# Expert rounds of a diffusion trunk on one core: where column pieces, gathers and turns stand on TensorE, an unrolled loop, and two smaller edits

## The chip, the core and the metric

The program runs on one core of a Trainium2 chip. The core has five engines that run their own instruction queues and meet only at semaphores: TensorE (PE in the profile; PEld is its weight load), VectorE (DVE), ScalarE (ACT), GpSimd (POOL) and SyncE (SP, which here issues nearly all loads). The metric is device time in microseconds of one execution, lower is better. All data is float32.

## The reference, cut to what matters

One inference step over two groups of 128 tokens (context and latent), width 1024, four layers. Each layer has a token mixer (layers 0 and 3: gated DeltaNet; 1: short convolution; 2: neighbourhood attention) and a channel mixer: a dense SwiGLU in layers 0 and 2, and eight SwiGLU experts with two chosen for each token in layers 1 and 3.

```python
def moe_ffn(h, router, w_gu, w_down):
    logits = (h @ router).astype(jnp.float32)
    top_v, top_i = lax.top_k(logits, TOP_K)                       # 2 of 8
    w = jax.nn.softmax(top_v, axis=-1)
    combine = jnp.sum(jax.nn.one_hot(top_i, N_EXPERTS, dtype=jnp.float32) * w[..., None], axis=-2)
    gu = jnp.einsum('btd,edf->btef', h, w_gu)                     # 1024 x 2*1408 for each expert
    g, u = jnp.split(gu, 2, axis=-1)
    act = jax.nn.silu(g) * u * combine[..., None].astype(h.dtype)
    return jnp.einsum('btef,efd->btd', act, w_down)               # 1408 x 1024 for each expert

def dense_ffn(h, w_gu, w_down):
    g, u = jnp.split(h @ w_gu, 2, axis=-1)
    return (jax.nn.silu(g) * u) @ w_down
```

In the DeltaNet mixer, `g` is summed along each chunk (`g = jnp.cumsum(...)`), and differences of these sums go through an exponential into the decay matrix. After each channel mixer comes a gated residual and, ahead of the next mixer, an RMS norm.

## The kernel before

**The expert layers.** Each of the two runs eight rounds, one for an expert. In a round the tokens of that expert are gathered (`gather`: multiplications of the token rows with a selection matrix into banks 7 and 2 of the accumulator, which ACT and DVE then copy into `xg`), multiplied with the expert's gate and up weights, gated, turned, and multiplied with the down weights. Rounds 0, 2, 4 and 6 hold up to 96 tokens (`body`), rounds 1, 3 and 5 up to 64 (`small`), and what is left over goes through `wide` with 128. A round's weights are 1408 gate and 1408 up columns and 1408 down rows.

They lie in eleven slots of a ring. Slots 0, 4, 6 hold 384 gate columns each (`GATE`), 1, 5, 7 the up columns (`UP`), 8, 9, 10 three blocks of 128 down rows each, and slots 2 and 3 (`GATE_D`, `UP_D`) the last 256 gate or up columns together with one block of down rows. In a `body` round the matmuls on 384 columns use three of the four 32-column strips of the array, and the fourth strip works on the last 256 columns at the same time: so `columns(q, 0, ...)`, the first piece of a round, already needs slot 2, and the second needs slot 3 (`landed(q, j_d)`).

SP issues the loads of the next round in the fixed order 0, 1, 4, 5, 2, 3, 6, 7, 8, 9, 10, each as soon as TensorE has counted the slot free (`p_gu` counts column pieces, `p_dn` down pieces). There is one set of slots, so a load is issued while the round before is still computed, and SP stands at the first slot that is not free.

**The order on TensorE** is the order of the program. In `body` it is: columns of piece 0, columns of piece 1, `turn(0)`, `down(0)`, columns of piece 2, `turn(1)`, `down(1)`, both gathers for the next round, `turn(2)`, `down(2)`, `down(3)`. `turn(s)` transposes the gated block `s` (three transposes into bank 6); ACT copies it to `ma_T` and raises `a_at`; `down(s)` waits for that copy. So there is a wait for ACT wherever `down(s)` stands right behind `turn(s)`. In `small` the four column pieces are followed by `turn_small(0)`, `down_small(0)`, both gathers, `turn_small(1)`, `down_small(1)`. Round 0 is straight code, rounds 1 to 4 are two turns of a hardware loop (`pe.Fori(1, NARROW - 2, 2)`, one `small` and one `body` in a turn), rounds 5 and 6 are straight code again. ACT and DVE have loops of the same shape.

**The dense layers.** The last `down` adds into banks 2 to 5 in order (`k` 0 to 7, two to a bank) and raises `unit_done` at its end. DVE waits for this and then makes the residual bank by bank (`residual`, four instructions each, `xT`), ACT squares each finished bank for the norm, and TensorE sums the squares.

**DeltaNet.** `s_gc` makes, for one head, four 128x128 blocks whose rows all hold the running sum of the gates: a multiplication of a broadcast column of `G_` with a triangular matrix. The same running sums are in `GC` by then. DVE reads the blocks in `s_dec` (line 1985).

## Time and profile before

| what | value |
|---|---|
| median of 3 runs | 2390.7 us (2389.5 to 2394.16) |
| the profiled execution, its own time | 2388.28 us |
| its span | 2386.4 us |
| TensorE busy in it | 2247.8 us (94%) |
| DVE / ACT / POOL busy | 483.6 / 394.4 / 66.9 us |
| mean granted TensorE clock | 0.976 of full speed |
| moved by DMA | 551.00 MB, 231 GB/s over the span |

The profiled execution is 2.4 us below the median of the runs; 1.9 us of its own time lie outside its span. The expert rounds of layer 1 lie between 790 and 1202 us, those of layer 3 between 1979 and 2376 us. The dense layers end at 644 and 1645 us, and the DeltaNet cores lie between 192 and 365 us and between 1781 and 1912 us.

How to read the rows below. A timeline row has the start of a group of instructions, the time from its first start to its last end, engine, line, operation, shapes and count; the bracket is the idle time of the engine just before and what ended it. Nearly all matmuls pass through one helper and so have line 636; a float32 multiplication shows as two records there, a transpose as one. Turns have the lines 1134, 1135, 1173, 1175, 1236 and 1275. A row of windows has, for a stretch, its length and the busy time of each engine, then the granted TensorE clock, the share of the DMA engines and GB/s. "issue" is a wait that no semaphore in the profile explains.

### The profile page before, as it was taken

The page shows a single profiled execution, that of the slowest core. Times are in us where ns is not written, and L with a number is a line of the kernel's source. Part 1 is how long each engine was busy: PE and PEld are TensorE (multiplying, and loading weights), DVE is VectorE, ACT ScalarE, POOL GpSimd, SP SyncE. Part 2 cuts the span into 40 slices and gives each one's busy share as a digit, 9 for nine tenths or more (in the row PEclk, how much of TensorE's full clock was granted, in tenths as well). Part 3 has the DMA queues.
Part 4 walks back from the last instruction along what each step waited for, and adds up shares of the span by engine and source line. Part 5 has one row for each costly group of instructions (what it writes and reads, how often), then busy time and mean ns, then how long its engine had stood idle before and what let it go on. Part 6 is the DMA issues. An engine that isn't in the chain of part 4 may idle for free.

```text
span 2386.4 us, 44001 instructions
## 1 busy us (share of the span) xinstructions
PE 2247.8 (94%) x19595; PEld 1615.6 (68%) x19595; DVE 483.6 (20%) x1376; ACT 394.4 (17%) x819; POOL 66.9 (3%) x109
## 2 busy tenths in 40 slices
PE   7999998999999998999999999999998989989998
PEld 4776666888888544445576578888878875444455
DVE  2234332000112400000111420002344423000002
ACT  1133223000100100000112320001143331000001
POOL 4000001000000000000000000000000000000000
PEclk8999999999999999999999899999999989999999
DMA  8967888743355499999575696413440056999991
GB/s 323 279 226 280 304 312 270 211 153 115 106 168 203 158 384 353 368 380 382 206 237 193 223 258 185 139 36 108 142 138 7 12 177 246 386 369 373 380 389 56
DMA packets 355915, 551.00 MB, mean 231 GB/s; under 512 B 11280, under 2 KB 311184, under 8 KB 343232
## 3 DMA queue, kind: packets, MB, share of 16 engines
q1 hardware_dynamic: 344352, 525.31, 63.3%
q0 software_dynamic: 5840, 18.11, 2.9%
q10 hardware_dynamic: 5536, 4.73, 0.6%
q8 instruction: 160, 2.62, 0.5%
q14 instruction: 27, 0.22, 0.0%
HBM read 537.64 MB, written 14.93 MB: 232 GB/s over the span
## 4 chain that ended last, share of the span: by engine, by line
PE 88%; DVE 5%; ACT 3%; issue 2%; DMA 2%; ACTq 0%; SPq 0%; DVEq 0%
PE ps L636 86%; ACT ring L1437 1%; ACT work L1437 1%; DMA ring<-in_moe_w_down 1%; DVE ring L2003 0%; DVE work L1844 0%; DVE ring L1985 0%; DVE ring L2008 0%; DVE ring L1993 0%; DMA ring<-in_ada_w 0%; PE ps L1134 0%; PE ps L1027 0%; DVE ring L2011 0%; DVE xT L1862 0%; PE ps L662 0%
## 5 line engine op out<-in xcount | busy, mean ns | idle before, releaser
L636 PE MATMUL ps<-ring,work 128*32 128x384 f32 (+6 forms) x7752 | 698.3, 450 | 50.5 <-ACT work L1437 24.3
L636 PE MATMUL ps<-hT,ring 128*128 128x256 f32 x3200 | 713.2, 382 | 3.4 <-DVE hT L1854 3.2
L636 PEld LDWEIGHTS ps<-hT,ring 128*128 128x128 f32 x3200 | 608.4, 191 | 112.9 <-issue 12.2
L636 PEld LDWEIGHTS ps<-ring,work 128*32 128x32 f32 (+2 forms) x7752 | 336.1, 115 | 388.8 <-issue 264.1
L1437 ACT ACTIVATE work<-ps 128x256 f32<-128x256 f32 (+5 forms) x244 | 103.1, 436 | 1363.0 <-PE ps L636 1186.8
L636 PE MATMUL ps<-work,ring 128*128 128x256 f32 (+1 forms) x1344 | 289.7, 375 | 10.9 <-DVE work L2070 6.3
L636 PEld LDWEIGHTS ps<-work,ring 128*128 128x128 f32 (+1 forms) x1344 | 243.1, 188 | 47.4 <-DVE work L2070 7.9
L636 PE MATMUL ps<-ring 64*64 64x64 f32 (+1 forms) x4192 | 182.7, 229 | 18.9 <-ACT ring L1437 7.2
L636 PEld LDWEIGHTS ps<-ring 64*64 64x64 f32 x4192 | 160.1, 138 | 57.8 <-ACT ring L1437 24.2
L1437 ACT ACTIVATE ring<-ps 128x512 f32<-128x512 f32 (+3 forms) x208 | 101.6, 491 | 342.7 <-PE ps L636 331.5
L636 PE MATMUL ps<-work 128*128 128x128 f32 (+2 forms) x736 | 104.9, 296 | 4.3 <-DVE work L2190 4.2
L636 PEld LDWEIGHTS ps<-work 128*128 128x128 f32 (+1 forms) x736 | 94.8, 202 | 17.5 <-issue 14.3
L2398 DVE TENSOR_TENSOR work<-work,ps 128x256 f32<-128x256 f32 x44 | 18.5, 421 | 420.9 <-ACT work L1437 420.9
L636 PE MATMUL ps<-ring,csil 128*2 128x512 f32 x768 | 98.9, 603 | 3.7 <-DMA ring<-in_ada_w 3.7
L1862 DVE SCALAR_TENSOR_TENSOR xT<-ps,mods,xT 128x128 f32<-128x128 f32 x160 | 43.6, 345 | 142.4 <-PE ps L636 120.2
L2336 DVE TENSOR_TENSOR work<-work,ps 96x128 f32<-96x128 f32 x24 | 6.8, 284 | 251.5 <-PE ps L636 227.6
L636 PE MATMUL ps<-ring,cst 64*64 64x64 f32 (+1 forms) x320 | 46.6, 313 | 10.6 <-ACT ring L1437 10.6
L2019 DVE TENSOR_TENSOR ring<-ps,cst 128x256 f32<-128x256 f32 x80 | 33.3, 423 | 96.9 <-PE ps L636 96.3
L1437 ACT ACTIVATE hT<-xT 128x512 f32<-128x512 f32 x32 | 19.8, 628 | 142.3 <-DVE xT L1862 142.3
L1881 DVE SCALAR_TENSOR_TENSOR ring<-ring,par 128x256 f32<-128x256 f32 x96 | 42.3, 482 | 1.7
L1879 DVE TENSOR_SCALAR ring<-ring,par 128x256 f32<-128x256 f32 x48 | 14.8, 352 | 133.2 <-ACT ring L1437 133.2
L636 PE MATMUL ps<-hT,cst 128*128 128x256 f32 x128 | 33.8, 422 | 6.6 <-ACT hT L1437 6.6
(263 smaller groups left out, 953.6 us busy)
## 6 DMA issues: line engine op xcount, KB each, us to landing
ring<-in_moe_w_gu SPq DMA_DIRECT2D x96, 1536.0 KB, 14.5
ring<-in_ada_w SPq DMA_DIRECT2D x96, 1024.0 KB, 7.1
ring<-in_moe_w_down SPq DMA_DIRECT2D x48, 1536.0 KB, 16.4
ring<-in_ff_w_gu SPq DMA_DIRECT2D x88, 512.0 KB, 5.7
ring<-in_dn_w_in SPq DMA_DIRECT2D x32, 1024.0 KB, 5.5
ring<-in_moe_w_gu SPq DMA_DIRECT2D x32, 1024.0 KB, 8.7
ring<-in_ff_w_down SPq DMA_DIRECT2D x44, 512.0 KB, 6.8
ring<-in_moe_w_down SPq DMA_DIRECT2D x32, 512.0 KB, 10.6
```

The costliest lines, as they stand in the source:

```text
L636: return pe.matmul(out, lhsT, rhs, start=start, stop=stop, **kw)
L1437: return act.activation(out, in_, fn, **kw)
L1862: ins = stt(xT[:, k, g * P:(g + 1) * P], ps[:, bank, c * NT + g * P:c * NT + (g + 1) * P], mods[:, l, col + k, g:g + 1], xT[:, k, g * P:(g ...
L1879: ins = ts(v(ys[c]), x, ws[c](tap), None, ALU.mult)
L1881: ins = stt(v(ys[c]), x, ws[c](tap), v(ys[c]), ALU.mult, ALU.add)
L2019: tt(four(MW(l, w)), ps[:, X, 0:4 * HB].rearrange("p (d g n) -> p d g n", d=2, g=2), level(lev), ALU.mult).then_inc(d_m, 1)
L2336: tt(ma_s[0:CAP, s, DW:GW], mg_s[0:CAP, DW:GW], ps[0:CAP, PU[s], DW:GW], ALU.mult)
L2398: tt(act_s[:, j % 3, :], gate_s[:, j % 3, :], ps[:, FB[j % 3], NT:2 * NT], ALU.mult) \
```

## The change

1. `body`: the columns of piece 2 are split around `down(0)`, one of the two gathers stands between `turn(1)` and `down(1)`, the other between `turn(2)` and `down(2)`. In the last round there are no gathers, and these two pairs stay together.
2. `small`: `turn_small(0)` moves ahead of the last column piece, `turn_small(1)` between the two gathers. A wait for `d_act` that the next turn has anyway is dropped.
3. `wide`: the columns of `GATE_D` and `UP_D` stand between `turn_wide(0)` and `down_wide(0)`, `turn_last` ahead of `down_wide(1)`, and the transposes of the stored rows (`stored`) ahead of `down_wide(2)`.
4. TensorE's loop over rounds 1 to 4 is unrolled. ACT's and DVE's loops stay.
5. SP waits for `p_dn` as well ahead of loading `GATE_D`. In the rounds that wait was there already.
6. Dense layers: the last `down` raises `p_last` after each of the first three banks, and DVE's residual waits bank by bank.
7. DeltaNet `s_gc`: a transpose of the broadcast column of `GC` in place of the multiplication.

```diff
@@ SP
                     if m in GU_FREE:
                         sp.wait_ge(moe["p_gu"], done[0] * 6 + (GU_FREE[m] - 6))
+                        if m == GATE_D:
+                            sp.wait_ge(moe["p_dn"], done[0] * 4 - 3)
...
                                 sp.wait_ge(moe["p_gu"], (done[0] + r) * 6 + GU_FREE[j])
+                                if j == GATE_D:
+                                    sp.wait_ge(moe["p_dn"], (done[0] + r) * 4 + 1)
                                 if j in (GATE_D, UP_D):
                                     sp.wait_ge(moe["p_dn"], (done[0] + r) * 4 + 1)
@@ TensorE: s_gc
-                        ins = mm(cols(X, c), sv(G_, 32)[:, k:k + 1].to_broadcast([P, P]), tri[d])
+                        ins = pe.transpose(cols(X, c), sv(GC, 32)[:, k:k + 1].to_broadcast([P, P]), ident)
@@ TensorE: gate_up
-                    if s == 2:
-                        pe.wait_ge(moe["d_act"], q * 3 + 1)
@@ TensorE: small
                     columns_small(q, ((GATE[2], GW), (GATE_D, DW)), PG[1], 1)
+                    turn_small(q, 0)
                     columns_small(q, ((UP[2], GW), (UP_D, DW)), PU[1], 1)
-                    turn_small(q, 0)
                     down_small(q, 0)
-                    pe.wait_ge(moe["d_act"], q * 3 + 3)
                     pe.wait_ge(moe["d_g"], q + (i + 2))
                     gather(0)
+                    turn_small(q, 1)
                     gather(1)
-                    turn_small(q, 1)
                     down_small(q, 1)
@@ TensorE: wide
                     turn_wide(q, 0)
-                    down_wide(q, 0)
                     whole(q, GATE_D, 7, 0, DW)
                     whole(q, UP_D, 7, DW, DW).then_inc(moe["p_gd"], 1)
+                    down_wide(q, 0)
                     gate_up_wide(q, 2)
                     turn_wide(q, 1)
                     stored(q, 0)
                     stored(q, 1)
+                    turn_last(q)
                     down_wide(q, 1)
-                    turn_last(q)
                     turn_back(q)
                     turn_wide(q, 2)
-                    down_wide(q, 2)
                     stored(q, 2)
                     stored(q, 3)
+                    down_wide(q, 2)
                     down_wide(q, 3)
@@ TensorE: body
                     turn(q, 0)
+                    columns(q, 2, GATE[2], GATE_D, PG[2])
                     down(q, 0, first)
-                    gate_up(q, 2, first)
+                    columns(q, 2, UP[2], UP_D, PU[2])
                     turn(q, 1)
-                    down(q, 1, first)
                     if not last:
                         pe.wait_ge(moe["d_g"], q + (i + 2))
                         gather(0)
+                    down(q, 1, first)
+                    turn(q, 2)
+                    if not last:
                         gather(1)
-                    turn(q, 2)
                     down(q, 2, first)
                     down(q, 3, first)
@@ TensorE: the rounds
-                with pe.Fori(1, NARROW - 2, 2) as r:
+                for r in range(1, NARROW, 2):
                     small(q0 + r)
-                    body(q0 + r + 1, False)
-                small(q0 + (NARROW - 2))
-                body(q0 + (NARROW - 1), False, True)
+                    body(q0 + r + 1, False, r == NARROW - 2)
@@ TensorE: the last down of a dense layer
+                        if stop and k in (1, 3, 5):
+                            ins.then_inc(p_last, 1)
                     return ins.then_inc(unit_done, 1)
@@ DVE: the residual of a dense layer
-                dve.wait_ge(unit_done, PLAN.first[l]["ffn"] + SLOTS * revs)
                 for b in range(4):
+                    if b < 3:
+                        dve.wait_ge(p_last, 3 * (l // 2) + b + 1)
+                    else:
+                        dve.wait_ge(unit_done, PLAN.first[l]["ffn"] + SLOTS * revs)
                     residual(l, b, 2 + b, 40)
```

TensorE, second half of round 0 (a `body`) in layer 1, before. Three transposes into `ps` are a turn, `ring,work 32x256 x35` is a down piece, `work 128x128` are the gathers, and `m_a_at` is ACT's copy of the turned block:

```order
L1134 MATMUL ps<-cst,work 128x128 [waits m_a_at,m_d_act]
L1134 MATMUL ps<-cst,work 128x128
L1135 MATMUL ps<-cst,work 128x96
L636 MATMUL ps<-ring,work 32x256 [waits moe_in9,m_a_at]
L636 MATMUL ps<-ring,work 32x256 x35
L636 MATMUL ps<-work 128x128 [waits m_d_g]
L636 MATMUL ps<-work 128x128 x15
L1134 MATMUL ps<-cst,work 128x128 [waits m_a_at,m_d_act]
L1134 MATMUL ps<-cst,work 128x128
L1135 MATMUL ps<-cst,work 128x96
L636 MATMUL ps<-ring,work 32x256 [waits moe_in10,m_a_at]
```

The same place now:

```order
L1137 MATMUL ps<-cst,work 128x128 [waits m_a_at,m_d_act]
L1137 MATMUL ps<-cst,work 128x128
L1138 MATMUL ps<-cst,work 128x96
L641 MATMUL ps<-work 128x128 [waits m_d_g]
L641 MATMUL ps<-work 128x128 x7
L641 MATMUL ps<-ring,work 32x256 [waits moe_in9,m_a_at]
L641 MATMUL ps<-ring,work 32x256 x35
L1137 MATMUL ps<-cst,work 128x128 [waits m_a_at,m_d_act]
L1137 MATMUL ps<-cst,work 128x128
L1138 MATMUL ps<-cst,work 128x96
L641 MATMUL ps<-work 128x128 x8
L641 MATMUL ps<-ring,work 32x256 [waits moe_in10,m_a_at]
```

Each gather now stands between a turn and the down piece that needs the turned block.

TensorE, between the end of round 0 and round 1 in layer 1, before; `L1350` is the loop:

```order
L636 MATMUL ps<-ring,work 32x256 x59
L1350 UNCONDITIONAL_BRANCH
L1350 ISA
L1104 ISA [waits m_d_xg,m_a_xg]
L636 MATMUL ps<-ring,work 32x384 [waits moe_in4,moe_in0]
L636 MATMUL ps<-ring,work 32x384 x31
```

The same place now:

```order
L641 MATMUL ps<-ring,work 32x256 x59
L641 MATMUL ps<-ring,work 32x384 [waits moe_in0,moe_in4,m_d_xg,m_a_xg]
L641 MATMUL ps<-ring,work 32x384 x31
L641 MATMUL ps<-ring,work 32x384 [waits moe_in5,moe_in1]
L641 MATMUL ps<-ring,work 32x384 x31
```

The branch is gone, and in layer 1 the waits are for constants.

DVE at the end of layer 0's dense part, before:

```order
L1862 SCALAR_TENSOR_TENSOR xT<-ps,mods,xT 128x128 [waits unit_done]
L1862 SCALAR_TENSOR_TENSOR xT<-ps,mods,xT 128x128 x15
L1844 TENSOR_TENSOR work<-xT,work 128x512 [waits a_rs]
L1844 TENSOR_TENSOR work<-xT,work 128x512
L1854 TENSOR_SCALAR hT<-work,gscs,mods 128x128 [waits d_nx]
```

The same place now (the first two rows stand there three times):

```order
L1866 SCALAR_TENSOR_TENSOR xT<-ps,mods,xT 128x128 [waits p_last]
L1866 SCALAR_TENSOR_TENSOR xT<-ps,mods,xT 128x128 x3
...
L1866 SCALAR_TENSOR_TENSOR xT<-ps,mods,xT 128x128 [waits unit_done]
L1866 SCALAR_TENSOR_TENSOR xT<-ps,mods,xT 128x128 x3
L1848 TENSOR_TENSOR work<-xT,work 128x512 [waits a_rs]
```

Three of the four banks no longer wait for the end of the last `down`.

## Rows read from the trace of the kernel before

**Rows 1.** Waits of TensorE: engine, line, waited for: us, times, longest; narrow rounds, layer 1

```profile
PE ps L636 <- ACT work L1437: 10.5, 18, 0.7
PE ps L636 <- issue: 10.1, 3, 5.5
PE ps L636 <- DMA ring<-in_moe_w_down: 2.1, 1, 2.1
```

**Rows 2.** The page's groups of DMA issues: the gate and up loads of 1536 KB

```profile
ring<-in_moe_w_gu SPq DMA_DIRECT2D x96, 1536.0 KB, 14.5
```

**Rows 3.** Windows in the rounds of layer 1; last three numbers: clock, DMA share, GB/s

```profile
836.00:936.00 100.00, 96.45 (x1226) 49.98 (x1225) 7.00 (x18) 8.42 (x20) 0.00 (x0) 1.00 1.06 382
936.00:980.00 44.00, 33.52 (x350) 15.80 (x350) 2.68 (x7) 3.15 (x7) 0.00 (x0) 0.88 0.90 323
980.00:1075.00 95.00, 90.20 (x1111) 43.39 (x1103) 6.99 (x18) 7.95 (x19) 0.00 (x0) 1.00 1.06 382
```

**Rows 4.** Windows in the rounds of layer 3

```profile
2124.00:2160.00 36.00, 29.17 (x321) 11.79 (x314) 1.98 (x6) 2.12 (x5) 0.00 (x0) 0.91 0.98 352
2160.00:2259.00 99.00, 94.41 (x1150) 47.20 (x1148) 7.69 (x19) 8.99 (x21) 0.00 (x0) 1.00 1.06 382
```

**Rows 5.** Timeline of TensorE, layer 1, rounds 2 to 6

```profile
905.30 14.41 PE L636 MATMUL ps<-ring,work 128*32 128x256 f32 x200 [0.64 <-ACT work L1437]
...
941.62 1.49 PE L636 MATMUL ps<-ring,work 128*32 128x384 f32 x4 [5.50 <-issue]
946.83 21.65 PE L636 MATMUL ps<-ring,work 128*32 128x384 f32 x252 [3.72 <-issue]
...
969.62 5.36 PE L636 MATMUL ps<-ring,work 128*32 128x512 f32 x48 [0.66 <-ACT work L1437]
...
1058.47 5.36 PE L636 MATMUL ps<-ring,work 128*32 128x512 f32 x48 [0.58 <-ACT work L1437]
...
1075.17 22.54 PE L636 MATMUL ps<-ring,work 128*32 128x384 f32 x256 [2.06 <-DMA ring<-in_moe_w_down]
```

**Rows 6.** Timeline of TensorE, layer 3: second turn of the loop, start of round 6

```profile
2130.70 9.67 PE L636 MATMUL ps<-ring,work 128*32 128x384 f32 x96 [6.17 <-issue]
...
2258.97 20.84 PE L636 MATMUL ps<-ring,work 128*32 128x384 f32 x256 [1.01 <-DMA ring<-in_moe_w_down]
```

**Rows 7.** Timeline of TensorE, `wide` of layer 1

```profile
1151.98 22.64 PE L636 MATMUL ps<-ring,work 128*128 128x512 f32 x76 [0.66 <-ACT work L1437]
...
1181.76 0.52 PE L1236 MATMUL ps<-cst,work 128*128 128x128 f32 x3 [0.35 <-ACT work L1437]
1182.86 5.42 PE L636 MATMUL ps<-ring,work 128*128 128x512 f32 x12 [0.58 <-ACT work L1437]
```

**Rows 8.** Timeline at the ends of the dense parts, layers 0 and 2

```profile
644.01 4.23 DVE L1862 SCALAR_TENSOR_TENSOR xT<-ps,mods,xT 128x128 f32<-128x128 f32 x16 [6.07 <-PE ps L636]
...
651.29 0.47 ACT L1437 ACTIVATE work<-ps,eps 128x256 f32<-128x256 f32 x1 [2.40 <-PE ps L636]
...
1639.74 5.56 PE L636 MATMUL ps<-work,ring 128*128 128x256 f32 x25
...
1651.45 0.47 ACT L1437 ACTIVATE work<-ps,eps 128x256 f32<-128x256 f32 x1 [1.22 <-PE ps L636]
```

**Rows 9.** Timeline around `s_gc` (`cst,sm`) and turns, layers 0 and 3

```profile
190.49 1.04 PE L751 MATMUL ps<-cst,work 128*128 128x128 f32 x8
...
228.79 1.04 PE L636 MATMUL ps<-ring,csil 128*2 128x512 f32 x8
...
1807.67 2.05 PE L636 MATMUL ps<-cst,sm 128*128 128x128 f32 x16
...
1808.86 2.16 DVE L1985 SCALAR_TENSOR_TENSOR ring<-ps,sm,cst 128x128 f32<-128x128 f32 x8 [2.52 <-PE ps L636]
...
1811.41 1.15 PE L636 MATMUL ps<-ring 64*64 64x64 f32 x32 [0.61 <-DVE ring L2019]
```

**Rows 10.** Window with turns and the first `s_gc` of layer 0

```profile
187.00:197.00 10.00, 7.81 (x63) 6.26 (x62) 6.09 (x20) 5.72 (x10) 0.00 (x0) 1.00 0.58 211
```

More of the change, by code:

```diff
@@ L279, in trunk @@
             sem("p_" + n) for n in ("gc", "kk", "ks", "w", "ut", "y", "z", "tz", "o"))
+        p_last = sem("p_last")
         p_s, p_pt, p_av = sem("p_s"), sem("p_pt"), sem("p_av")
```

## The prediction, written before the changed kernel had run

> **What bounds the kernel now.** I read the page first (TensorE busy 94%), then TensorE's waits and its timeline in the rounds, then the windows for the transfers. In the narrow rounds of layer 1, from 794 to 1126 us, TensorE waits 10.5 us for ACT in 18 places, 10.1 us for "issue" in three and 2.1 us for a weight load in one [rows 1]. So it looks like TensorE's stage with small holes. The windows say more: in every long stretch of the rounds the DMA share is above 1 and the rate is 382 GB/s, the same number three times over 294 us in two layers [rows 3, 4]. That is a ceiling, and the loads run at it nearly always. The reader should see the one place where they do not: 936 to 980 us (323 GB/s) and 2124 to 2160 us (352 GB/s) [rows 3, 4]. There TensorE stood in the loop's second turn [rows 5, 6], freed no slots, and SP had nothing to issue.
>
> Compare what two rounds need. TensorE: from the second half of round 3 (969.62) to that of round 5 (1058.47) is 88.85 us with no stall but the waits for ACT [rows 5]. The loads: 22 x 1536 KB, which is 34.6 MB [rows 2], and about 0.8 MB of stores and instructions (my allowance), 35.4 MB, at 382 GB/s 92.7 us. So the loads are slower than TensorE by some 4 us in two rounds. TensorE can be ahead only because of the credit that the loop's stall gave it; by round 6 the credit is used up, and TensorE waits for a load: 2.06 us in layer 1, 1.01 us in layer 3 [rows 5, 6]. The load named is that of slot 2, which a `body` needs at its first piece. From here the rule for the whole change: **what TensorE saves before the start of round 6 is worth nothing in itself; what counts is when the loads get there.** After that start, the weights of the last two rounds land ahead of their use and TensorE's own time sets the end.
>
> **The change part by part.**
>
> *Waits behind turns, before round 6.* Each goes: turn 0 is followed by a column piece of about 5 us (20.84 us for four [rows 6]), turns 1 and 2 by a gather of about 2 us, against a wait of 0.58 us on average (10.5/18) [rows 1]. That is 3 waits in each of rounds 0, 2, 4 and 2 in each of 1, 3, 5, 15 waits, 8.7 us a layer, of TensorE's time. Two rounds now take it 88.85 - 5 x 0.58 = 85.9 us, against 92.7 for the loads. So the saving turns into a wait of about 7 us for slot 2 at rounds 4 and 6. Worth on the path: only that the slots of round 0 come free about 0.5 us earlier, before the loads are saturated. 0.5 us a layer.
>
> *The loop.* With the branch back gone, the stalls of 5.50 + 3.72 us (layer 1) and 6.17 us (layer 3) go [rows 5, 6]. Their value is the transfer time that was lost: (382 - 323)/382 x 44 = 6.8 us in layer 1 and (382 - 352)/382 x 36 = 2.8 us in layer 3 [rows 3, 4]. What is late next is the load of slot 2 itself. Whether straight code is fetched without stalls the rows can't prove for all rounds; bounds are 0 and one stall of 9.2 us for each round. I take 0: rounds 0, 5 and 6 are straight code under the same 382 GB/s, and the only "issue" waits in the narrow rounds are three, two of them at the branch and the third under 1 us [rows 1, 5]. ACT and DVE keep their loops; if their branch stalls alike, TensorE has the last down pieces and 15 us of column pieces before it needs them.
>
> *Round 6 and `wide`.* Here TensorE's savings count. In round 6 only the wait behind turn 0 goes (0.6 us): without gathers `turn(1)`, `down(1)` and `turn(2)`, `down(2)` stay neighbours. In `wide` the three waits of 0.66, 0.35 and 0.58 us go [rows 7], each behind at least a microsecond of transposes or a column piece: 1.6 us. Together 2.2 us a layer.
>
> *The clock.* A long wait costs more than itself. Round 6's first four pieces took 22.54 us in layer 1 after 2.06 us idle, and 20.84 us in layer 3 after 1.01 us idle [rows 5, 6]; the granted clock was below full speed over the loop's stall too (0.88) [rows 3]. With a wait of about 7 us at round 6 layer 3 loses what layer 1 loses already, 1.7 us; layer 1 stays as it is. Bounds: 0 (the clock holds) and 3.4 us a layer (the loss doubles with the wait). At rounds 2 and 4 such a loss is hidden, since TensorE waits for the loads anyway.
>
> *SP.* The added wait asks for the same count as the one behind it; the loads that queue behind it (2, 3, 6, 7, ...) wait for nothing new. `down(1)` ends a gather (2 us) later, so slot 8 is freed later; loads of more than 10 us are in flight then (14.5 us from issue to landing [rows 2]). Both 0.
>
> *The dense parts.* The last `down` is 16 records of 0.22 us (25 in 5.56 us [rows 8]), 0.9 us a bank, so the first bank is complete 2.6 us ahead of the end. DVE's sixteen instructions take 4.23 us; they now end 1.6 us behind the last matmul and not 4.2. ACT's step on the finished sum starts 7.3 us after the end in layer 0 (644.0 to 651.29) and 6.15 us after it in layer 2 (1645.30 to 1651.45) [rows 8]; the first had the half clock in its sums, which needs the idle time that now goes. I take 3.7 and 2.6 us, 6.3 together. Nothing else is queued on DVE there. Bounds 4 and 7.
>
> *`s_gc`.* Eight multiplications take 2.05 us, eight transposes 1.04 [rows 9]. No row shows a transpose of a broadcast column; the nearest are these, so a pair of heads costs between 1.04 and 2.05 us, and I take 1.04. In layer 3 the path runs through the first head of the pair into DVE (2.16 us) and back to TensorE, which waits 0.61 us [rows 9]: half the saving counts, 0.5 us, four times. In layer 0 panels of 1.04 us stand between and hide DVE's part, so I take 0.85 us three times and 0.5 us once. Sum 5.0 us; bounds 0 and 8.
>
> A reading of the Trainium skill can be weighed here. The row gives a transpose half the time of a multiplication, 1.04 to 2.05 us. The Trainium skill, page "TensorE: Matmul & The Clock Gate", section "Terms", puts the transpose mode at four times as fast for FP32. By that page the edit would, as an estimate, give a pair of heads 0.51 us and the sum about 2.5 us more; the measured row decides.
>
> *Sum.* Layer 1's experts 6.8 + 0.5 + 2.2 = 9.5; layer 3's 2.8 + 0.5 + 2.2 - 1.7 = 3.8; dense 6.3; `s_gc` 5.0: 24.6 us. The profiled execution took 2388.3 us, so its successor 2363.7; the median of the runs is 2.4 us higher, so I predict 2366.
>
> **The rivals.**
>
> *TensorE is the bound all through.* Then all its waits are worth their length: 16 waits of 0.58 us and 1.6 us in `wide`, 10.9 us a layer; the loop's 9.2 and 6.2 us and some 2 us of half clock each; the two waits for loads, 1.0 us and 2.1 + 1.7 us. That is 46 us, with the other edits 57, time 2333. For it: 94% busy. Against it: the 382 GB/s. It would need transfers over 400 GB/s, and no stretch of 90 us has that.
>
> *The loads give nothing back.* If they go at 382 GB/s but later slots start late because TensorE waits, the 9.6 us of transfer time are lost in another place. Expert rounds then gain about 2 us, time 2377. For it: TensorE will wait near 7 us for slot 2, and frees nothing meanwhile. Against it: at that moment slots 2, 3, 6 to 10 are all issued, seven loads of 4.1 us, and the next slot comes free 5 us on.
>
> *Straight code is fetched too slowly* (the slower side). Rounds 3 to 6 of each layer are new code on TensorE. If each of those eight rounds began with a stall like the loop's, 7.7 us, two rounds would lose 15.4 us, of which the 7 us of waiting for slot 2 hide a part; 8 us are left in each of four pairs, 32 us. Time 2366 + 32 = 2398. It decides from the point where two rounds lose more than the 7 us. Against it stand rounds 0, 5 and 6 of now.
>
> *The transposes cost the clock.* If a group of transposes let the clock fall for a few microseconds, each of the eight `s_gc` groups would lose up to the 1.7 us of [rows 5, 6], 14 us: 2380. Against it: 187 to 197 us holds the eight transposes of [rows 9] and some 2 us of idle TensorE, and its clock is 1.00 [rows 10]. The Trainium skill, same page, section "Part 4: PE-mode transpose", says that a transpose doesn't count as busy TensorE in the same way; the trace of that stretch doesn't bear it out.
>
> *An edit does nothing:* `s_gc` or the dense part gains nothing because another engine is next. Each makes it 5 to 6 us less, 2371 to 2372.
>
> **How the numbers follow.** Forecast, its own spread included (2358 to 2373): 0.72. TensorE-bound wholly or in part: 0.07. Loads give nothing back: 0.12. Transposes' clock: 0.04. Slow fetch: 0.05. Range 2356 to 2378: it takes in the second rival and the bounds of the clock, the dense parts and `s_gc`, and leaves out the two large ones. A difference of 0.2%, 4.8 us, is about what a measurement of this kernel can tell from none. Faster 0.93 (all but slow fetch and a little), same 0.03, slower 0.04.
>
> **What the profile after would show.** TensorE's waits for ACT in a layer's narrow rounds fall from 18 to 2 or 3; "issue" loses its long waits; waits for expert weights rise from 3 us in the kernel to 25 to 35, at the first pieces of rounds 4 and 6 (smaller at 2), with a lower clock behind them. The rate stays 382 GB/s from 836 us to round 6 with no dip. Eight `s_gc` multiplications' 2.05 us read 1.04. DVE's residual starts before the dense part's last matmul ends. I am wrong if TensorE waits little for weights and the rounds are much shorter (first rival), if the rate has a new dip (second), or if "issue" waits stand in rounds 3 to 6 (third).

## The result, and the profile after

The changed kernel takes 2364.3 us in the median (2363.55 to 2364.86, 4 runs), the kernel before beside it 2390.1 us (2387.53 to 2394.16, 4 runs). The ratio is 0.989, its 95% interval 0.9873 to 0.9907. The forecast was 2366 us. The profiled execution of the changed kernel has a span of 2361.7 us and took 2363.55 us; the sum of the prediction had put it at 2363.7.

I read the profile after in the order of the steps. First TensorE's waits in the narrow rounds of layer 1 (engine, line, what it waited for, us in total, times, the longest):

```profile
PE ps L641 <- DMA ring<-in_moe_w_down: 12.8, 2, 7.2
PE ps L641 <- ACT work L1441: 1.1, 2, 0.6
PE ps L641 <- issue: 0.8, 1, 0.8
```

Against [rows 1], the 18 waits for ACT have become 2, the long "issue" waits are gone, and in their place stand two waits for expert weights: 22.7 us of waits became 14.7. In the whole kernel TensorE now waits 26.0 us for those weights. Where they stand is seen in its timeline (start, duration, what runs, and in brackets the idle time before it):

```profile
966.10 22.61 PE L641 MATMUL ps<-ring,work 128*32 128x384 f32 x256 [7.22 <-DMA ring<-in_moe_w_down]
...
1059.45 23.71 PE L641 MATMUL ps<-ring,work 128*32 128x384 f32 x256 [5.60 <-DMA ring<-in_moe_w_down]
...
1098.96 1.29 PE L641 MATMUL ps<-ring,work 128*32 128x256 f32 x20 [0.55 <-ACT work L1441]
...
2047.69 20.84 PE L641 MATMUL ps<-ring,work 128*32 128x384 f32 x256 [0.18 <-DMA ring<-in_moe_w_down]
...
2140.90 22.30 PE L641 MATMUL ps<-ring,work 128*32 128x384 f32 x256 [7.23 <-DMA ring<-in_moe_w_down]
...
2234.11 23.47 PE L641 MATMUL ps<-ring,work 128*32 128x384 f32 x256 [5.76 <-DMA ring<-in_moe_w_down]
```

Apart from the row at 1098.96 these are the first four column pieces of rounds 4 and 6 in layer 1 and of rounds 2, 4 and 6 in layer 3. The profile names the load with down rows as what ended each wait; slot 2, which holds such rows and is the one that the first piece needs, is my reading of that name. The row at 1098.96 is one of the waits that stay, behind turn 1 of round 6. Look at the durations too: the same 256 matmuls take 20.84 us behind no wait and up to 23.71 us behind a long one [rows 5, 6 have 22.54 and 20.84]. The windows of the same stretches (TensorE's clock, the DMA share and the GB/s are the last three numbers) show why that costs little so far:

```profile
830.00:936.00 106.00, 106.00 (x1363) 53.84 (x1365) 7.98 (x20) 8.24 (x20) 0.00 (x0) 1.00 1.05 384
936.00:980.00 44.00, 36.78 (x380) 17.48 (x375) 3.00 (x8) 2.99 (x8) 0.00 (x0) 0.92 1.06 381
980.00:1059.00 79.00, 73.85 (x921) 37.78 (x914) 5.68 (x15) 6.60 (x16) 0.00 (x0) 1.00 1.05 382
2005.00:2103.00 98.00, 97.81 (x1258) 49.45 (x1260) 7.42 (x19) 7.75 (x19) 0.00 (x0) 1.00 1.06 382
2103.00:2149.00 46.00, 38.77 (x413) 18.04 (x408) 2.94 (x7) 3.48 (x9) 0.00 (x0) 0.93 1.06 382
```

The stretch that had 323 GB/s [rows 3] has 381, and that with 352 [rows 4] has 382. TensorE still stands still there, but no longer for a branch: for weights, while the transfers run at their ceiling.

The other edits. `wide` of layer 1, around its turns:

```profile
1135.99 22.54 PE L641 MATMUL ps<-ring,work 128*128 128x256 f32 x76
1158.37 0.49 PE L1238 MATMUL ps<-cst,work 128*128 128x128 f32 x3
1158.70 1.04 PE L1250 MATMUL ps<-cst,work 128*128 128x128 f32 x8
1159.57 0.38 PE L1277 MATMUL ps<-cst,work 128*128 128x128 f32 x2
1159.79 5.32 PE L641 MATMUL ps<-ring,work 128*128 128x512 f32 x12
```

None of the three waits of [rows 7] is left. The end of the dense part of layer 0:

```profile
631.96 7.07 PE L641 MATMUL ps<-work,ring 128*128 128x256 f32 x32
...
636.47 4.23 DVE L1866 SCALAR_TENSOR_TENSOR xT<-ps,mods,xT 128x128 f32<-128x128 f32 x16 [3.48 <-PE ps L641]
...
642.58 0.47 ACT L1441 ACTIVATE work<-ps,eps 128x256 f32<-128x256 f32 x1 [1.22 <-PE ps L641]
```

DVE starts 2.56 us before the last matmul ends (631.96 + 7.07 = 639.03), and ACT's step on the finished sum comes 3.55 us behind it, where it was 7.3 [rows 8]. TensorE's sums of squares in between, before and then after, show what the gain is made of:

```profile
645.85 5.41 PE L636 MATMUL ps<-hT,cst 128*128 128x256 f32 x16 [1.88 <-ACT hT L1437]
```

```profile
638.86 3.68 PE L641 MATMUL ps<-hT,cst 128*128 128x256 f32 x16
```

The wait of 1.88 us is gone, and the sixteen records behind it take 1.7 us less. In layer 2 they took 4.23 us before and 3.68 after. The kernel before had a granted clock of 0.76 over these sums in layer 0 (644.0 to 651.2 us) and of 1.00 in layer 2: the 1.2 us by which layer 0 gains more are the clock, the other 2.6 waiting.

And `s_gc` in layer 0, then in layer 3:

```profile
223.42 1.09 PE L809 MATMUL ps<-cst,sm 128*128 128x128 f32 x8
...
264.69 1.09 PE L809 MATMUL ps<-cst,sm 128*128 128x128 f32 x8
...
1789.27 1.09 PE L809 MATMUL ps<-cst,sm 128*128 128x128 f32 x8
...
1820.43 1.09 PE L809 MATMUL ps<-cst,sm 128*128 128x128 f32 x8
```

A group takes 1.09 us, not 2.05 [rows 9]; the window of [rows 10] still has its full clock:

```profile
187.00:197.00 10.00, 7.82 (x67) 5.55 (x69) 6.98 (x22) 5.52 (x10) 0.00 (x0) 1.00 0.56 211
```

**Where the time came from.** The two executions are laid beside each other at equal places of TensorE's program; what a stretch became shorter is what it gave. The places are the first matmuls of groups that are easy to recognize (round 0's first column piece, `wide`'s first one, a norm's second group), since single records can be missing from a trace and a count of records then slips:

| stretch | before, us | after, us | given | predicted |
|---|---|---|---|---|
| layer 0, first norm to the second | 393.3 | 388.5 | 4.8 | 3.1 |
| norm to norm over the dense part, layer 0 | 238.6 | 234.8 | 3.8 | 3.7 |
| layer 1, first column piece of round 0 to that of `wide` | 335.6 | 327.8 | 7.8 | 7.9 |
| layer 1, `wide` to the next layer's first projection | 72.8 | 70.5 | 2.3 | 1.6 |
| norm to norm over the dense part, layer 2 | 237.4 | 234.8 | 2.6 | 2.6 |
| layer 3, DeltaNet | 136.7 | 135.3 | 1.4 | 2.0 |
| layer 3, round 0 to `wide` | 329.2 | 327.7 | 1.5 | 2.2 |
| layer 3, `wide` to the end | 74.3 | 72.5 | 1.8 | 1.6 |

That is 26.0 us against a span shorter by 24.7; 1.3 us net went elsewhere, in places that no edit touches: 1.3 us between the dense part of layer 0 and round 0 of layer 1, 1.7 us ahead of layer 3's DeltaNet core, and 1.5 us came back behind that core.

### The profile page after: what moved, and what is told of

The parts are those of the page before. It is cut to its first block, busy times and chain, and to the rows that moved or that the text cites. A ratio compares the mean times of both kernels' runs of the same rounds, so it can differ in the third digit from the quotient of the medians.

```text
span 2361.7 us, 43842 instructions
## 1 busy us (share of the span) xinstructions
PE 2241.4 (95%) x19531; PEld 1614.3 (68%) x19531; DVE 483.8 (20%) x1376; ACT 393.0 (17%) x819; POOL 66.9 (3%) x109
## 4 chain that ended last, share of the span: by engine, by line
PE 85%; DVE 5%; DMA 3%; SPq 3%; ACT 2%; issue 1%; ACTq 0%; DVEq 0%
PE ps L641 83%; SPq L481 3%; DMA ring<-in_moe_w_down 2%; ACT ring L1441 1%; DVE ring L1989 1%; ACT work L1441 1%; DVE ring L2007 0%; DVE work L1848 0%; PE ps L1137 0%; DVE ring L2012 0%; DVE ring L1997 0%; PE ps L1032 0%; DMA ring<-in_ada_w 0%; DVE ring L2015 0%; PE ps L667 0%
## 5 line engine op out<-in xcount | busy, mean ns | idle before, releaser
L641 PE MATMUL ps<-work,ring 128*128 128x256 f32 (+1 forms) x1344 | 289.7, 375 | 10.9 <-DVE work L2074 6.3
L641 PEld LDWEIGHTS ps<-ring,cst 64*64 64x64 f32 (+1 forms) x320 | 20.9, 154 | 26.0 <-ACT ring L1441 22.5
```

The source lines that it names most:

```text
L641: return pe.matmul(out, lhsT, rhs, start=start, stop=stop, **kw)
```

## The experiments

All times are medians; the kernel before that stands beside a run ran on the same chip.

| kernel | us | runs | before, us | ratio, 95% interval |
|---|---|---|---|---|
| loop unrolled alone | 2382.2 | 12 | 2386.95 | 0.9968 to 0.9991 |
| order alone | 2378.4 | 6 | 2386.95 | 0.9940 to 0.9969 |
| `s_gc` alone | 2376.4 | 6 | 2386.95 | 0.9936 to 0.9965 |
| dense edit alone | 2386.7 | 12 | 2386.95 | 0.9973 to 1.0001 |
| changed kernel, second time | 2362.2 | 4 | 2386.9 | 0.9879 to 0.9911 |
| filled ahead of round 6 | 2360.3 | 5 | 2386.9 | 0.9874 to 0.9906 |
| filled ahead of round 4 | 2363.5 | 4 | 2386.9 | 0.9883 to 0.9915 |
| changed, lighter loads | 2327.4 | 4 | 2386.9 | 0.9741 to 0.9773 |
| before, lighter loads | 2378.4 | 6 | 2387.1 | 0.9955 to 0.9980 |
| changed without the dense edit | 2368.5 | 6 | 2389.5 | 0.9896 to 0.9933 |
| filled ahead of round 6, second time | 2361.0 | 6 | 2389.5 | 0.9863 to 0.9907 |
| changed kernel, third time | 2364.1 | 6 | 2389.5 | 0.9883 to 0.9921 |

### The loop unrolled alone

```diff
-                with pe.Fori(1, NARROW - 2, 2) as r:
+                for r in range(1, NARROW, 2):
                     small(q0 + r)
-                    body(q0 + r + 1, False)
-                small(q0 + (NARROW - 2))
-                body(q0 + (NARROW - 1), False, True)
+                    body(q0 + r + 1, False, r == NARROW - 2)
```

> The kernel before with TensorE's loop over rounds 1 to 4 unrolled and nothing else changed. Theory (the loads set the start of round 6): the stalls of 9.2 and 6.2 us disappear from TensorE, but only the transfer time lost to them comes back, 6.8 us in layer 1 and 2.8 us in layer 3; TensorE then waits some 4 us for slot 2 at rounds 4 and 6, and round 6 of layer 3 loses up to 1.7 us to the lower clock: 8 us in all, 2382 us. Rival (TensorE is the bound): the stalls and half clock go whole, about 19 us, 2371 us. Rival (straight code fetched with stalls): issue waits at the starts of rounds 3 to 6, no gain.

Measured 4.75 us less in the median (2382.2 us is the expected figure only because the kernel before stood at 2387 us beside it). From the first column piece of round 0 to that of `wide` the trace is 6.1 us shorter in layer 1, and in layer 3 not at all (0.0). Windows of layer 1 and the first four pieces of round 6 in both layers:

```profile
836.00:936.00 100.00, 96.46 (x1237) 49.13 (x1239) 7.42 (x19) 9.02 (x21) 0.00 (x0) 1.00 1.06 382
936.00:980.00 44.00, 40.94 (x460) 18.84 (x456) 2.95 (x7) 3.69 (x9) 0.00 (x0) 1.00 1.06 383
```

```profile
1065.97 23.23 PE L636 MATMUL ps<-ring,work 128*32 128x384 f32 x256 [4.18 <-DMA ring<-in_moe_w_down]
...
2246.95 23.24 PE L636 MATMUL ps<-ring,work 128*32 128x384 f32 x256 [4.03 <-DMA ring<-in_moe_w_down]
```

The dip in the transfers is gone (383 for 323 GB/s), and TensorE waits the predicted 4 us for slot 2 at round 6 (1.80 and 1.54 us at round 4, where 4 were expected too). It stood idle 15.4 us less for the branch, and the rounds gave 6.1 us: somewhat less than the theory's 8, and far from the first rival's 19. Where the 2 us went can be read off. Round 6 starts 7.6 us earlier in layer 1 and 3.3 in layer 3, measured from round 0: that is the lost transfer time, worked out as 6.8 and 2.8. Behind that start the lower clock took 0.7 us in layer 1 (23.23 us for 22.54 [rows 5]) and 2.4 in layer 3 (23.24 for 20.84 [rows 6]; the theory allowed 1.7), and the wait for ACT's copy ahead of `wide` grew by 0.8 and 0.9 us. No wait at "issue" of more than 1 us stands in the rounds, so straight code is not fetched slowly here; that was the third rival.

### The new order alone

```diff
                     turn(q, 0)
+                    columns(q, 2, GATE[2], GATE_D, PG[2])
                     down(q, 0, first)
-                    gate_up(q, 2, first)
+                    columns(q, 2, UP[2], UP_D, PU[2])
                     turn(q, 1)
-                    down(q, 1, first)
                     if not last:
                         pe.wait_ge(moe["d_g"], q + (i + 2))
                         gather(0)
-                        gather(1)
+                    down(q, 1, first)
```

(cut here; the second gather moves behind `turn(q, 2)`, and the like happens in `small` and `wide`, with the waits that go with it)

> The new order in the rounds alone, with TensorE's loop kept and neither the dense edit nor that of the s_gc rows. Theory: TensorE reaches the loop's stall earlier, so that some 4 us (layer 1) and 2.8 us (layer 3) of transfer time come back, 1 us from the earlier slots, 4 us in round 6 and the wide rounds, less 2 us of lower clock: about 10 us, 2380 us; with the unrolling alone that is more than the 13 us of both together. Rival (TensorE is the bound, all terms add): 22 us, 2368 us.

Measured 8.6 us less. From round 0 to `wide` layer 1 gave 4.6 us and layer 3 1.2 us; the last stretch of the kernel gave 1.5. The loop's stall stayed (5.49 and 3.92 us in layer 1), yet the rate in its window rose. I read this as the theory had it, TensorE reaching the stall earlier and having freed more slots by then:

```profile
936.00:980.00 44.00, 39.69 (x408) 18.40 (x411) 2.94 (x7) 2.94 (x7) 0.00 (x0) 0.89 0.99 357
```

It was 323 GB/s [rows 3] and is 357. Do the two edits add? In the medians they seem to (4.75 + 8.6 = 13.3, about what both were to give). Up to the start of round 6 in the traces they don't: in layer 1 it comes 7.6 and 5.2 us earlier, 12.8 apart, and 8.3 with both edits; in layer 3 3.3 and 2.8, 6.1 apart, and 3.5 with both. Both draw on the same transfer time.

### `s_gc` as transposes, alone

```diff
-                        ins = mm(cols(X, c), sv(G_, 32)[:, k:k + 1].to_broadcast([P, P]), tri[d])
+                        ins = pe.transpose(cols(X, c), sv(GC, 32)[:, k:k + 1].to_broadcast([P, P]), ident)
```

> The s_gc rows turned as transposes (and nothing else of the change). Theory: 5 us gone in the two DeltaNet layers, 2385 us, with the granted clock as before. Rival: transposes leave TensorE at the lower clock in more stretches, no gain or a loss.

Measured 10.6 us less, twice what was expected, and the trace shows that half of it has nothing to do with `s_gc`. The parts that the edit touches gave what was foreseen: layer 0 from norm to norm 3.6 us, layer 3's DeltaNet core 1.6, together 5.2 for 5.0. Between the second and the third group in layer 0 lie 42.07 us before and 41.26 now (0.8 given, 0.85 predicted), in layer 3 31.66 and 31.15 (0.5 given, 0.5 predicted). But the rounds of layer 1, which this edit does not touch, are 6.0 us shorter. One reason is this row, the first behind the loop's branch:

```profile
938.43 23.23 PE L636 MATMUL ps<-ring,work 128*32 128x384 f32 x256 [5.49 <-issue]
```

The second of the two stalls of [rows 5], 3.72 us, is missing. Why it is, the trace doesn't say: it may be chance or where the code now lies; I did not test that. The other reason: round 6 began at full clock (20.84 us behind a wait of 1.41 us, against 22.54 behind 2.06 [rows 5]). The rival, a lower clock behind transposes, is out: the window 187 to 197 us has 1.00 here too.

### The dense edit alone, and the change without it

```diff
+                        if stop and k in (1, 3, 5):
+                            ins.then_inc(p_last, 1)
...
-                dve.wait_ge(unit_done, PLAN.first[l]["ffn"] + SLOTS * revs)
                 for b in range(4):
+                    if b < 3:
+                        dve.wait_ge(p_last, 3 * (l // 2) + b + 1)
+                    else:
+                        dve.wait_ge(unit_done, PLAN.first[l]["ffn"] + SLOTS * revs)
                     residual(l, b, 2 + b, 40)
```

> The dense layers' residual edit alone. Theory: 3.7 us and 2.6 us at the ends of the two dense layers, 6.3 us in all, 2384 us. Rival: what follows waits for something else, under 3 us.

Measured 0.3 us less, with 12 runs from 2375.5 to 2393.4 us: by the median the theory had fallen. But the profiled execution of it took 2392 us with the dense end of layer 0 3.8 us shorter all the same. What it lost, it lost elsewhere, 5.1 us of it between `wide` of layer 1 and the second norm of layer 2. Here are 75 us of layer 2, this kernel and then the kernel before:

```profile
1290.00:1365.00 75.00, 64.91 (x339) 38.33 (x339) 27.73 (x69) 28.40 (x77) 4.24 (x5) 0.77 0.48 165
```

```profile
1290.00:1365.00 75.00, 65.32 (x395) 39.72 (x394) 30.02 (x77) 29.95 (x83) 4.24 (x5) 0.89 0.55 192
```

A granted clock of 0.77 against 0.89, in code that is the same in both. So I took the edit away from the changed kernel instead, whose runs lie closer together.

> The changed kernel without its dense edit: the residual of a dense layer again waits for the whole last unit. The dense edit alone moved the median little, while in its one trace the ends of the dense layers came 3.8 us earlier in layer 0. Theory (the edit is worth its 6.3 us, the median of the run alone was spread by stretches of lower clock elsewhere): 6 us more than the changed kernel beside it, about 2369 us, and between equal places of the two traces 3.8 us at the end of layer 0 and 2.6 us at that of layer 2. Rival (the edit is worth nothing in the median): 2363 us.

Measured 2368.5 against 2364.1 us beside it: 4.4 us more, nearer to the theory's 6 than to nothing, though the intervals of the two ratios overlap. Between equal places of the two traces the dense part of layer 0 is 3.9 us longer and that of layer 2 3.8 us (2.6 were expected; this time the sums of squares had the lower clock in both layers, 0.77 and 0.76 over them, and took 5.58 and 5.41 us). The traces say that the edit is worth at least what it was said to be; a median of twelve runs did not show it.

### Filling TensorE's wait

```diff
                     small(q0 + r)
+                    if r == NARROW - 2:
+                        for _ in range(11):
+                            mm(ps[:, 6, 0:2 * P], ident, cst[:, C_ID:C_ID + 2 * P])
                     body(q0 + r + 1, False, r == NARROW - 2)
```

In the kernel filled ahead of round 4 the condition is `r == NARROW - 4`.

> The changed kernel again, a yardstick for the variants of it that run beside it: 2364 us.

Measured 2362.2 us.

> The changed kernel with 11 extra matmuls on the identity (about 5 us, into an unused bank) ahead of round 6, where TensorE waits 5.6 and 5.8 us for expert weights anyway. Theory (the wait leaves TensorE at the lower clock for the first matmuls of round 6): the first four pieces of round 6 take 20.9 us and not 23.7 and 23.5, 5.5 us gone, 2359 us. Rival (the weights set the time there, or the filling delays the round): no gain, or up to 2 us lost.

Measured 2360.3 us, 1.9 less than its neighbour. In the trace the mechanism is all there. The end of round 5 and the start of round 6 in layer 1:

```profile
1056.43 5.01 PE L641 MATMUL ps<-cst 128*128 128x256 f32 x22
1062.16 20.84 PE L641 MATMUL ps<-ring,work 128*32 128x384 f32 x256 [0.72 <-DMA ring<-in_moe_w_down]
```

The first row is the filling. The wait of 5.60 us is 0.72, and the four pieces take 20.84 us for 23.71. Windows over the same 14 us, filled and then unfilled, have a clock of 1.00 and 0.80 at the same rate of transfers (367 and 366 GB/s), so it is not the traffic that makes these pieces slow:

```profile
1050.00:1064.00 14.00, 13.28 (x105) 8.36 (x107) 1.39 (x2) 1.22 (x3) 0.00 (x0) 1.00 1.06 367
```

```profile
1050.00:1064.00 14.00, 8.40 (x70) 3.08 (x65) 0.85 (x2) 0.59 (x1) 0.00 (x0) 0.80 1.07 366
```

From the first piece of round 4 to `wide` the trace is 2.8 us shorter in each layer than that of the changed kernel beside it, 5.6 for an expected 5.5. The median shows a third of that.

> The same 11 extra matmuls ahead of round 4 and none ahead of round 6. Theory (between rounds 4 and 6 the loads set the time, so the lower clock of round 4 is hidden): no gain, 2364 us. Rival (TensorE's clock there counts): 3 us gone, 2361 us.

Measured 2363.5 us: 1.3 more than the changed kernel beside it and 3.2 more than the kernel filled ahead of round 6. As a test it is weak, since the filling did not keep the clock there: 2.19 us of idle time were left, and the four pieces still took 22.5 us.

```profile
2135.10 5.01 PE L641 MATMUL ps<-cst 128*128 128x256 f32 x22
2142.31 22.54 PE L641 MATMUL ps<-ring,work 128*32 128x384 f32 x256 [2.19 <-DMA ring<-in_moe_w_down]
```

What the clock of round 4 is worth is better read from two other kernels. In layer 3 of the unrolled kernel the first four pieces of round 4 take 20.84 us, in the changed one 22.30; from there to the first piece of round 6 both need 93.2 us. The 1.5 us are hidden.

> The changed kernel with the 11 extra matmuls ahead of round 6, again. In its first trace the stretches from round 5 to the wide rounds were 2.7 and 2.9 us shorter than in the changed kernel, and 2.8 us were lost before, in layer 0. Theory (the loss in layer 0 is chance, the gain is not): 5 us less than the changed kernel beside it. Rival (the loss in layer 0 belongs to the longer program): 2 to 3 us less.

> The changed kernel once more, the yardstick that stands beside these runs on the same chip: 2363 us, as twice before.

Measured 2361.0 and 2364.1 us: 3.1 less. From round 4 to `wide` the traces give 2.3 and 2.8 us. This time layer 0 cost no more than in the first profile of the changed kernel, and it was the changed kernel itself that lost 2.9 us there: its second and third norm came at 410.5 and 645.3 us, in its first profile at 407.6 and 642.4. So the loss of the first time does not need the longer program: chance, as the theory said. Part of it is an "issue" wait that the first profile hasn't:

```profile
307.15 0.68 PE L641 MATMUL ps<-ring 64*64 64x64 f32 x15 [1.06 <-issue]
```

But the filled kernel's second profile lost its gain in layer 2, where 1290 to 1350 us had a clock of 0.72 against 0.89 in its neighbour. Over both occasions it has 11 runs with a mean 3.0 us below that of the changed kernel's 10, with a standard error of 1.4: the best of these kernels, by more than chance, and by less than the 5.1 to 5.6 us that the traces of the rounds show. The theory's 5 us isn't reached, and the 2 to 3 us of the rival are what the medians say. I leave open whether the filling brings other stretches of lower clock with it.

### Lighter loads

```diff
-                def expert(e, j):
+                def expert(e, j, full=True):
...
                     else:
-                        down(3 * j - 22, 3, 0)
+                        down(3 * j - 22, 3 if full else 1, 0)
...
-                            expert(e, j)
+                            expert(e, j, False)
```

These two kernels leave out two of the three down blocks of slots 8 to 10 from the second round on, so their outputs are not the reference's. TensorE's program is the same: 19531 matmuls are in the profile of the changed kernel with either loads, and 19595 in that of the kernel before.

> The changed kernel whose expert slots 8, 9 and 10 load one of their three down blocks from round 2 of each expert layer on, so that a round loads 14.2 MB and not 17.3 (these blocks are then left over from earlier, the computation takes them as they are). Theory (the loads set rounds 4 and 6): the 26 us of waits for expert weights and up to 8.7 us of lower clock behind them go, and the time is about 2330 us. Rival (something else stands behind the weights, another wait takes over): waits of 5 us and more stay in these rounds, and the time is above 2345 us.

Measured 2327.4 us, for 2330 expected. Not one wait for expert weights is left:

```profile
830.00:1045.00 215.00, 215.00 (x2667) 108.48 (x2669) 16.61 (x43) 17.85 (x44) 0.00 (x0) 1.00 0.96 339
```

TensorE is busy in all of these 215 us, at full clock, with transfers at 339 GB/s. Nothing else stood behind the weights. From the first piece of round 4 to that of round 6 it takes 85.8 us in both layers; in the changed kernel it is 93.3 and 93.2 us, in all six profiles of it and of its filled variants 93.2 to 93.5. TensorE's own pace for two rounds had been worked out as 85.9 us, that of the loads as 92.7.

> The kernel before with the lighter loads of the run before (slots 8, 9 and 10 load one of their three down blocks from round 2 on). Theory (before the change TensorE sets the pace of the rounds, the loads stand behind it): only its two waits for weights (3.1 us) and 1.7 us of lower clock can go, about 2385 us, so that with light loads the change is worth about 55 us instead of 24. Rival (the loads set the rounds before the change as well): about 2350 us, a like gain to that of the changed kernel.

Measured 2378.4 us. So with light loads the change is worth 51 us, with the real ones 25: half of what TensorE saves goes into waiting for weights and into the clock behind the waits. The kernel before gained 8.7 us, not 2 to 5: the two waits for weights and layer 1's lower clock were the 5, and the loop's stalls were shorter, by 3.3 us in layer 1 and 1.2 in layer 3. Its waits in the narrow rounds of layer 1:

```profile
PE ps L636 <- ACT work L1437: 10.5, 18, 0.7
PE ps L636 <- issue: 6.8, 3, 4.7
```

6.8 us at "issue" where it was 10.1 [rows 1]. The windows of the first stall and of what follows it:

```profile
937.50:942.20 4.70, 0.04 (x4) 0.01 (x1) 0.42 (x1) 0.60 (x1) 0.00 (x0) 0.85 0.48 166
942.20:948.00 5.80, 4.51 (x28) 1.47 (x32) 0.00 (x0) 0.00 (x0) 0.00 (x0) 0.53 0.02 6
```

The transfers run out during the first stall, and it is 4.7 us long all the same, so full queues don't explain it. Whether they explain the 3.3 us that are missing I did not test; in the kernel with `s_gc` alone the second stall was missing with the queues full.

## Why the prediction was right, point by point

- **The bound.** "What TensorE saves before the start of round 6 is worth nothing in itself" held. Round 6 starts 272.3 and 272.6 us after round 0 in the changed kernel and 273.0 and 272.7 in the unrolled one, which still has all the waits behind its turns: 8.7 us a layer of TensorE's time moved that start by 0.7 and 0.1 us. Shown further by the unrolling alone (15.4 us of stalls removed, 6.1 given), by the two rounds' 93.3 us, whatever TensorE does in them, against 85.8 with lighter loads, and by the 51 us that the change gives with those for 25. The filling ahead of round 6 shows the other half, that time behind that start counts (5.6 us). The first rival, TensorE as the bound, falls with the same; so does the second, since the lost transfer time came back: from round 0 to the start of round 6 the change gave 8.3 us in layer 1 and 3.5 in layer 3, for 7.3 and 3.3. (The second rival's own time is off by a little: its terms, 24.6 less 9.6 us, make 2375.7 and not 2377.)
- **The waits behind the turns.** 18 to 2 as foreseen, and 26.0 us of waits for weights in the foreseen 25 to 35, at rounds 4 and 6. At round 2 of both layers the wait is nearly nothing (0.18 us in layer 3).
- **The clock.** The step was right, its size was not: this is the term of the sum that was mis-sized. I took 1.7 us for layer 3 and none for layer 1. Layer 3 lost 2.6 (20.84 to 23.47) and layer 1 another 1.2 (22.54 to 23.71). The runs give the size, since nearly every kernel of the study has such a row: these 256 matmuls, behind a wait for weights. With 0.18 to 1.80 us of wait they took 20.84 us in each of 13 rows; with 2.06 to 2.43 us 22.4 to 22.5 (three rows); with 4.0 to 4.7 us 23.0 to 23.2 (three); with 5.4 to 5.8 us 23.5 to 23.8 (ten); with 6.49 us 23.11 (one); with 7.1 to 7.5 us 22.3 to 22.6, save one of 23.65 (twelve). So the loss does not double with the wait, and behind the longest waits it is smaller again. Windows of the changed kernel's wait of 7.22 us at round 4 of layer 1 show why:

```profile
960.80:962.80 2.00, 0.00 (x0) 0.00 (x0) 0.00 (x0) 0.00 (x0) 0.00 (x0) 1.00 1.07 368
962.80:966.10 3.30, 0.00 (x0) 0.03 (x1) 0.00 (x0) 0.00 (x0) 0.00 (x0) 0.51 1.09 370
```

The last 3.3 us of the wait already have the lower clock, so a part of the slow time passes while TensorE does nothing. The bounds of 0 to 3.4 held. (The first row of [rows 6] stops at the end of its window; behind that stall of 6.17 us all 256 took 22.56 us.)
- **`wide` and round 6.** 2.3 and 1.8 us in the traces for 1.6: somewhat more than the three waits of [rows 7].
- **The dense parts.** 3.8 and 2.6 us for 3.7 and 2.6. Shown by adding the edit (3.8 and 2.6 us in its trace) and by taking it away (3.9 and 3.8). That layer 0's sums of squares lose their lower clock with the idle time, as foreseen, stands in the rows of 5.41 and 3.68 us.
- **`s_gc`.** 0.8 us per pair in layer 0 and 0.5 in layer 3 between groups, as worked out; layer 0 as a whole gave 1.7 us more than the term, layer 3 0.6 less. The former is less than the 2.9 us by which two executions of the changed kernel differ in layer 0.
- **Straight code and transposes' clock.** Neither rival showed: no long "issue" wait in the rounds, 1.00 in the window of [rows 10].

The sum came out within 0.2 us of the profiled execution. That closeness is luck: the clock took 2.1 us more than its term, the start of round 6 came 1.2 us earlier than foreseen, layer 0 gave 1.7 more, and 1.3 us net went in places that no edit touches; such things cancelled.

## What to carry to other kernels

Where transfers run at their ceiling, time the loads and TensorE over the same two rounds before counting what an idle gap is worth; a gap ahead of a place that the loads fix is free, the same gap behind it costs its length and the clock after it. Price a stall under full transfers as the transfer time it loses, by the dip in GB/s (9.6 us foreseen for the loop, 10.9 measured up to the start of round 6), and what follows it by the clock. And judge an edit of 5 us by equal places of two traces, or by taking it away from the kernel that scatters less; alone its median said 0.3 us for one such edit and 10.6 for another, where the traces said 6.4 and 5.2. Choose as equal places the first matmuls of groups that can be recognized.

## What I had not expected of the hardware

- The clock scatters with chance. One program, the dense edit alone, ran from 2375.5 to 2393.4 us, with a mean granted clock of 0.979 in the fastest and 0.972 in the slowest execution. The two levels are 1.2 and 2.4 GHz. Layer 2's 1290 to 1365 us had 0.77 in one kernel and 0.89 in another with the same code there; three executions of the changed kernel had 0.88, 0.88 and 0.89 from 1290 to 1350 us, so how far a given stretch scatters is open.
- 5 us of matmuls on the identity in a wait are paid back: the next 256 matmuls took 2.9 us less.
- The stall at a branch back of TensorE's loop, 5.5 us and then 3.7 us with transfers at their ceiling, was 4.7 and 1.3 us with lighter loads, though the transfers had then run out (6 GB/s behind the first stall), and in one kernel its second part was missing altogether with no edit near it.
